# Scan begun under the receptance and gate projections, and the head norm of a key tile placed inside the next tile's product

## The chip, the core and the metric

The kernel runs on one core of one Trainium2 chip. The metric is the device time of one execution in microseconds (us). A core has TensorE (PE, matrix products), VectorE (DVE), ScalarE (ACT) and GpSimd (POOL), which compute, and SyncE (SP), which here only issues DMAs. ACT and POOL issue DMAs too. Each engine works its own instructions in the order written; semaphores are the only links between engines.

## The reference, cut to what matters

The program is two small transformer models in a row. The change lies in one layer of the first, an RWKV-7 layer on 512 image tokens and 256 context tokens of width 1024 (16 heads of 64):

```python
xx = h_shift - h
xr, xw, xk, xv, xa, xg = [h + xx * mix[j] for j in range(6)]
r = xr @ wr
k = xk @ wk
v = xv @ wv
g = sigmoid(xg @ g1) @ g2
kk = to_heads(k * k_k)
kk = kk * rsqrt(sum(kk * kk, axis=-1, keepdims=True) + 1e-12)      # norm per head
for d in range(2):                                                # two directions
    decay = exp(-exp(-softplus(-(w0[d] + tanh(xw @ w1[d]) @ w2[d])) - 0.5))
    a = sigmoid(a0[d] + (xa @ a1[d]) @ a2[d])
    k_d = k * (1.0 + (a - 1.0) * k_a)
...
def step(s, inp):                                                 # the scan over tokens
    r_t, w_t, k_t, v_t, a_t, b_t = inp
    sa = einsum('bhvk,bhk->bhv', s, a_t)
    s = s * w_t + sa[..., None] * b_t[:, :, None, :] + v_t[..., None] * k_t[:, :, None, :]
    return s, einsum('bhvk,bhk->bhv', s, r_t)
```

Before the scan come a Fourier layer and a mixture of experts, after it the output projection, a second mixture of experts and the whole second model. None of these is touched.

## The kernel before, in words

Activations lie transposed: 128 features by tokens, eight such tiles (m = 0 to 7) for the width of 1024. All work of the layer before the scan is the stage `rw`, the scan is the stage `wkv`. Between two stages the helper `phase` makes each of PE, DVE and ACT wait until the other engines have ended the stage (POOL's part too).

Stage `rw` on PE (`rw_tensor`): the decay projection; then for each key tile m the product with `wk` (L986, 16 products written, which the trace counts as 32 matmuls: half have 512 columns, half 256), the four small products of the gate `a` (L998), and the head norm, two products of the squared key with a block matrix of ones (L1006). Then values (L1015, `wv`), receptance (L483, `wr`, eight tiles into the eight PSUM banks), and the output gate: `down("lg", "g1")` (L959) and the product with `g2` (L1027). The inputs of these projections are made by DVE in `mix` (L1070), six times, always into the same tile `XJ`; so each `mix` waits until the projection before it has read `XJ` (`xjfree`).

For a key tile m ACT (`rw_scalar`) copies the product out of PSUM (L1162), squares it (L1169, mark `ksq`), waits for DVE's results of tile m-1 and issues their five stores (L1134, on ACT's own DMA queue), computes two sigmoids of `a` in four instructions (L1175), and takes the square root of the head norm (L1179, mark `rn`). Sigmoid and square root are in different activation tables, so a table load stands before each. DVE (`rw_vector`) then needs the stores of tile m-1 landed and the sigmoids of m, makes the directions' keys (L1103, L1106), takes the reciprocal (L1109), and makes `kk` and its products (L1111, L1114, mark `kout`). PE's head norm waits for `ksq`.

The products of values, receptance and gate are copied out by ACT into staging tiles (L1203, L1206), and POOL stores them to HBM (L1223, L1214).

Stage `wkv` works the tokens in chunks of 64, two units (u, one for each direction) to a step, twelve steps. A unit needs its chunk's streams loaded from HBM into the region of `H` (six DMAs, L1385 on ACT's queue for step 0, L301 on SP's queue for later ones), constants (L1380 to L1382), a cumulative sum on DVE (L1448), exponentials on ACT (L1346, L1347), the scaled keys on DVE (L1458, L1462), the chunk products on PE (L1575, 32 matmuls a unit), their copies on ACT (L1359, L1361), six masks and one strict mask a unit on POOL (L1323, L1337), and a start on DVE (L1484, L1489). Then PE, ACT and DVE go through levels 1 to 5 of a triangular inverse: product L1588, copy L1370, product L1602, addition L1498, transpose L1503. Within a step the next step's sum, exponentials and products are already worked. For step 0 nothing stands before them, so all come one after another when `rw` has ended.

SP loads weights through a ring of eight slots (L2652). Its order is that of `weight_plan`; the first block of `wo` comes after the gate's weights, and `wkv_loads` behind it.

Of the kernel before, what the change touches and what calls it, by code (L numbers as in the profile page):

```python
# [135 lines left out]
def build(nc, a, out, table):  # L136
# [3 lines left out]
    with ctx:  # L140
# [53 lines left out]
        for i in range(5):  # L194
            sems[f"st{i}"] = semaphore(f"stage_tile_{i}_stored_by_pool")
            sems[f"sa{i}"] = semaphore(f"stage_tile_{i}_stored_by_scalar")
        for i in range(2):
# [87 lines left out]
        block = ctx.enter_context(nc.Block())  # L285

# [656 lines left out]
        last_mm = {}  # L943
# [4 lines left out]
        def rw_tensor(pe):  # L948
# [3 lines left out]
            def down(tag, wn, j, last_name):  # L952
                w = weight(pe, wn)
                for s0, sn in jsegs(j):
                    b = bank(pe, f"{tag}.{s0}")
                    for k in range(KT):
                        if later(pe, f"xj{j}.{k}"):
                            pe.wait_ge(*at(f"xj{j}.{k}"))
                        ins = pe.matmul(b[:, 0:sn], w[:, k, :], XJ[:, k, s0:s0 + sn], start=k == 0, stop=k == KT - 1)  # L959
# [18 lines left out]
            wa = weight(pe, "a2")  # L978
            for m in range(KT):
# [9 lines left out]
                if m % 2:  # L989
                    marks[f"wf.wk.{m // 2}"] = (T_, count[T_])  # L990
                for d in range(2):
# [8 lines left out]
                if m == KT - 1:  # L1000
                    marks["xjfree2"] = (T_, count[T_])
                for s0, sn in SEGS:
                    if later(pe, f"ksq.{m}"):
                        pe.wait_ge(*at(f"ksq.{m}"))
                    b = bank(pe, f"kn.{m}.{s0}")
                    did(T_, pe.matmul(b[:, 0:sn], bones[:, :], SQ[:, s0:s0 + sn], start=True, stop=True).then_inc(tensor_done, 1), f"kn.{m}.{s0}")  # L1006
# [14 lines left out]
            down("lg", "g1", 5, None)  # L1021
# [8 lines left out]
        def rw_vector(dve):  # L1030
# [32 lines left out]
            def mix(n):  # L1063
                j = order[n]
                if n:
# [3 lines left out]
                for k in range(KT):  # L1069
                    did(V, dve.scalar_tensor_tensor(XJ[:, k, 0:w], XX[:, k, 0:w], col("mix", 8 * j + k), H[:, k, 0:w],  # L1070
# [46 lines left out]
            mix(5)  # L1117

# [4 lines left out]
        def rw_scalar(act):  # L1123
# [68 lines left out]
            n = 0  # L1192
            for tag in ("v", "r", "g"):
                if tag == "g":
                    lora("lg", 0, ACT.Sigmoid, XSEG)
                for m in range(KT):
# [11 lines left out]
                    n += 1  # L1208

        def rw_pool(pool):  # L1210
# [15 lines left out]
            for tag in ("v", "r", "g"):  # L1226
# [8 lines left out]
            for step in [f"s.{x}.{KT - 1}" for x in ("kk", "kka0", "kka1", "kd0", "kd1")]:  # L1235
                if later(pool, step):
                    pool.wait_ge(*at(step))

# [8 lines left out]
        off = 0  # L1247
# [6 lines left out]
        YA = take_scr(KT, TX)  # L1254
# [5 lines left out]

        AR = [[take_scr(KT, 2, CH) for _ in range(2)],
# [51 lines left out]
        def wkv_pool(pool):  # L1313
# [12 lines left out]
            if later(pool, "wkvc"):  # L1326
                pool.wait_ge(*at("wkvc"))
# [1622 lines left out]
```

## Time and profile before

| | us |
|---|---|
| three runs, median | 4153.48 |
| lowest and highest | 4148.98, 4155.55 |
| the profiled execution, its own time | 4151.23 |
| its span, first to last instruction | 4149.3 |
| stage `rw`, from its first projection to the gate's last product | 1109 to 1467 |
| PE waits between the gate's last product and the first of the scan | 1467 to 1493 |
| scan, from the first chunk product to about | 1493 to 2002 |

The span is 1.9 us shorter than the execution's own time; what lies around it is taken to stay. Positions below are us from the span's start. A row of the timeline gives start, duration, engine, line, operation, what is written and read, and in brackets how long the engine was idle before and who ended that. The mean granted clock of TensorE is 0.956 of full speed, which is 2.4 GHz; the other level is half of it.

### The profile page before, as it was taken

Reading aid. Unit: us, or ns where it says so; the run is one execution under the profiler, and the core shown is the slowest. Engines: PE = TensorE matmul, PEld = TensorE weight load, DVE = VectorE, ACT = ScalarE, POOL = GpSimd, SP = SyncE. Lnnn points to the kernel's source line nnn. Section 1 sums busy time; section 2 is a strip of 40 time slices with the busy share of each in tenths; the row PEclk is TensorE's granted clock in tenths of the full one; section 3 lists DMA queues with packets and bytes.
Section 4 is the critical chain, followed back from the end, with each engine's and each line's share of the span. In section 5 each row is a group of like instructions: output and inputs, shape, how many; then the busy total and the mean of one; then the engine's idle time right before and its main releaser. Section 6 shows DMA issues by size and latency. Waiting matters only on the chain.

```text
span 4149.3 us, 63323 instructions
## 1 busy us (share of the span) xinstructions
PE 3711.9 (89%) x28370; PEld 2288.8 (55%) x28370; DVE 1350.4 (33%) x2376; ACT 1014.9 (24%) x1973; POOL 264.1 (6%) x240
## 2 busy tenths in 40 slices
PE   7998999999698969999768887779989998998998
PEld 3556443434355658888443332235548884656886
DVE  2123000000545047777430000025433332534243
ACT  3012111111232135554210000113323221423231
POOL 0000000000000034434100000000000000000000
PEclk9997999999888989999979999989999999999999
DMA  8345889896034154331519999911122322112230
GB/s 288 102 148 198 304 310 363 307 341 244 33 116 162 42 114 89 69 87 42 174 41 360 375 376 387 384 54 58 51 71 92 92 88 66 55 45 88 91 99 23
DMA packets 530414, 666.74 MB, mean 161 GB/s; under 512 B 156552, under 2 KB 299144, under 8 KB 530144
## 3 DMA queue, kind: packets, MB, share of 16 engines
q1 hardware_dynamic: 506352, 627.37, 44.6%
q10 hardware_dynamic: 19952, 22.81, 1.7%
q0 software_dynamic: 3840, 12.52, 0.8%
q8 instruction: 223, 3.65, 0.4%
q14 instruction: 47, 0.39, 0.0%
HBM read 631.18 MB, written 31.46 MB: 160 GB/s over the span
## 4 chain that ended last, share of the span: by engine, by line
PE 72%; DVE 10%; DMA 6%; SPq 4%; ACT 4%; POOL 2%; ACTq 1%; issue 1%; DVEq 0%; POOLq 0%
PE ps L620 11%; DMA ring<-in_moe_wu 5%; PE ps L625 4%; SPq L2652 4%; PE ps L483 3%; PE ps L813 3%; PE ps L2515 3%; PE ps L2516 3%; PE ps L2517 3%; PE ps L2531 3%; PE ps L2532 3%; PE ps L2530 3%; PE ps L786 3%; PE ps L2151 3%; PE ps L2257 3%; POOL ring L1323 2%
## 5 line engine op out<-in xcount | busy, mean ns | idle before, releaser
L620 PE MATMUL ps<-ring,H 128*64 128x512 f32 x2048 | 494.4, 602 | 52.4 <-DMA ring<-in_moe_wu 39.2
L620 PEld LDWEIGHTS ps<-ring,H 128*64 128x64 f32 x2048 | 146.9, 137 | 343.7 <-issue 253.9
L722 DVE TENSOR_TENSOR scr<-ps,scr 128x512 f32<-128x512 f32 x32 | 22.1, 691 | 965.2 <-PE ps L625 516.9
L620 PE MATMUL ps<-ring,scr 128*64 128x512 f32 x1024 | 248.3, 599 | 39.9 <-DMA ring<-in_moe_wd 38.5
L2515 PE MATMUL ps<-scr_rounded,ring_rounded 128*128 128x512 f32 x512 | 205.0, 400 | 23.0 <-ACT scr_rounded L2553 23.0
L2584 DVE TENSOR_TENSOR ring_rounded<-ring,scr_rounded 128x2048 fp32r<-128x2048 f32 x64 | 146.7, 2292 | 227.6 <-ACT scr_rounded L2550 227.6
L2516 PE MATMUL ps<-H_rounded,scr_rounded 128*128 128x512 f32 x512 | 204.8, 400 | 0.0
L2517 PE MATMUL ps<-scr_rounded 128*128 128x512 f32 x512 | 204.5, 399 | 0.0
L2532 PE MATMUL ps<-scr_rounded 128*128 128x512 f32 x512 | 202.6, 396 | 0.0
L2530 PE MATMUL ps<-scr_rounded,ring_rounded 128*128 128x512 f32 x512 | 202.0, 394 | 0.0
L2550 ACT ACTIVATE scr_rounded<-ring 128x2048 fp32r<-128x2048 f32 x64 | 122.1, 1908 | 257.7 <-PE ps L2532 246.4
L620 PEld LDWEIGHTS ps<-ring,scr 128*64 128x64 f32 x1024 | 73.0, 137 | 188.7 <-issue 125.0
L813 PE MATMUL ps<-scr 128*128 128x512 f32 (+1 forms) x320 | 125.9, 556 | 4.2 <-ACT scr L696 2.9
L786 PE MATMUL ps<-scr 128*128 128x256 f32 x512 | 121.3, 390 | 4.0 <-DVE scr L893 4.0
L2515 PEld LDWEIGHTS ps<-scr_rounded,ring_rounded 128*128 128x128 f32 x512 | 97.6, 191 | 48.5 <-DVE H_rounded L2589 24.6
L625 PE MATMUL ps<-ring,H 128*32 128x256 f32 x2048 | 123.8, 382 | 0.0
L690 ACT ACTIVATE scr<-ps 64x512 f32<-64x512 f32 x64 | 37.8, 591 | 312.6 <-PE ps L625 161.5
L2151 PE MATMUL ps<-H,ring 128*128 128x512 f32 x256 | 111.3, 594 | 0.0
L2516 PEld LDWEIGHTS ps<-H_rounded,scr_rounded 128*128 128x128 f32 x512 | 97.7, 191 | 23.7
L2257 PE MATMUL ps<-scr,ring 128*128 128x512 f32 x256 | 110.7, 593 | 0.0
L2517 PEld LDWEIGHTS ps<-scr_rounded 128*128 128x128 f32 x512 | 97.5, 190 | 23.6
L503 DVE SCALAR_TENSOR_TENSOR X<-ps,ada,X 128x512 f32<-128x512 f32 (+1 forms) x48 | 31.8, 662 | 241.7 <-PE ps L813 127.0
(405 smaller groups left out, 6246.1 us busy)
## 6 DMA issues: line engine op xcount, KB each, us to landing
ring<-in_moe_wg SPq DMA_DIRECT2D x128, 1024.0 KB, 9.2
ring<-in_moe_wu SPq DMA_DIRECT2D x128, 1024.0 KB, 8.4
ring<-in_moe_wd SPq DMA_DIRECT2D x128, 1024.0 KB, 11.3
ring<-in_mlp_w SPq DMA_DIRECT2D x64, 1024.0 KB, 5.5
ring<-in_ada_w SPq DMA_DIRECT2D x48, 1024.0 KB, 8.0
ring<-in_w_in SPq DMA_DIRECT2D x14, 1024.0 KB, 5.2
ring<-in_w_out SPq DMA_DIRECT2D x8, 1024.0 KB, 5.2
st_kka<-scr ACTq DMA_DIRECT2D x16, 384.0 KB, 3.5
```

The source lines that it names most:

```text
L620: ins = pe.matmul(bx[64 * n:64 * n + 64, :], stat_x(k), w[:, k % 4, :], start=k == 0, stop=k == KT - 1)
L625: ins = pe.matmul(bc[32 * n:32 * n + 32, 0:256], stat_c(k), w[:, k % 4, o:o + 256], start=k == 0, stop=k == KT - 1)
L786: ins = pe.matmul(b[:, 0:256], HT[:, tt, k * P:k * P + P], GM[:, tt, :], start=tt == 0, stop=tt == 3)
L813: ins = pe.matmul(b[:, 0:sn], ys[:, j, m * P:m * P + P], sm[:, j, :], start=j == 0, stop=j == nj - 1)
L2151: ins = pe.matmul(b, w[:, k, (m % 2) * P:(m % 2) * P + P], H[:, k, 0:TX], start=k == 0, stop=k == KT - 1)
L2257: ins = pe.matmul(banks[m], w[:, k, (m % 2) * P:(m % 2) * P + P], MIX[:, k, :], start=k == 5, stop=k == 4)
L2515: pe.matmul(b, low[:, k, o], hh, start=k == 0, stop=False)
L2516: pe.matmul(b, high[:, k, o], hl, start=False, stop=False)
L2517: ins = pe.matmul(b, high[:, k, o], hh, start=False, stop=k == KT - 1)
L2530: pe.matmul(banks[m], low[:, k, o], hh, start=f == 0, stop=False)
L2532: ins = pe.matmul(banks[m], high[:, k, o], hh, start=False, stop=f == 15)
L2652: did(f"slot{i % NSLOT}", sp.dma_start(dst, src.rearrange("(k p) c -> p k c", p=min(P, rows))).then_inc(sems[f"slot{i % NSLOT}"], 16), "w. ...
```

## The change

1. Keys: the head norm of tile m-1 (`head_norm`) is written between the 512-column and the 256-column part of tile m's product; that of the last tile stays behind its gate products. The order on ACT and DVE is not changed. The mark that frees `XJ` after the keys is set right after the last key product.
2. `mix` of the gate writes into `XX`, its own input, and so doesn't wait for the receptance projection to end.
3. Loads for step 0 go from ACT's queue to SP's (`wkv_first_loads`), behind the gate's weights and ahead of `wo`: constants once the receptance's inputs are made, the chunk streams once the gate's input is made, the values once the product with `g1` has read `XX`. The stores of the gate's tiles go from POOL to SP, in the same function, and so do the values of step 1.
4. DVE makes sum and scaled keys of step 0 right after `mix` of the gate; ACT makes the exponentials after the third receptance tile (`EXP_AFTER = 2`); PE works both chunk products between receptance and `g1`; ACT copies them out ahead of the gate's sigmoid; POOL masks them behind the stores of the receptance; DVE begins both units.
5. Tiles of the scan get other places in scratch memory, so that those needed early don't overlap what `rw` still uses. `AR` of even steps and of odd steps change places between `X` and scratch.

```diff
@@ wkv_first_loads, new, on SP, called ahead of the plan's "hold.0"
+            if later(sp, "xj5.0"):
+                sp.wait_ge(*at("xj5.0"))
+            did("wkvc", sp.dma_start(RST, a["rst"]).then_inc(sems["wkvc"], 16), by=16)
...
+            if later(sp, f"xj5.{KT - 1}"):
+                sp.wait_ge(*at(f"xj5.{KT - 1}"))
+            steps = list(units())
+            for u, d, c, img, first in steps[0]:
+                for n, s, h in chunk_streams(d, False):
...
+            if later(sp, "lg.0"):
+                sp.wait_ge(*at("lg.0"))
...
+            for u, d, c, img, first in steps[0]:
+                value_loads(sp, u, d, c)
+            for m in range(KT):
+                if later(sp, f"go.{m}"):
+                    sp.wait_ge(*at(f"go.{m}"))
+                did(f"sg{m % 4}", sp.dma_start(*stored("g", m, m % 4, TX)).then_inc(sems[f"sg{m % 4}"], 16), f"s.g.{m}", by=16)
+            for u, d, c, img, first in steps[1]:
+                value_loads(sp, u, d, c)
@@ rw_tensor
+            def head_norm(m):
+                if later(pe, f"ksq.{m}"):
+                    pe.wait_ge(*at(f"ksq.{m}"))
...
                 for s0, sn in SEGS:
+                    if s0 and m:
+                        head_norm(m - 1)
                     b = bank(pe, f"k.{m}.{s0}")
...
-                for s0, sn in SEGS:
-                    if later(pe, f"ksq.{m}"):
-                        pe.wait_ge(*at(f"ksq.{m}"))
...
+            head_norm(KT - 1)
...
-            down("lg", "g1", 5, None)
+            first_step = next(units())
+            chunk_products(pe, *first_step[0])
+            chunk_products(pe, *first_step[1])
+            down("lg", "g1", 5, None, XX)
@@ rw_vector
             mix(5)
...
+            first_step = next(units())
+            for un in first_step:
+                chunk_scan(dve, *un)
+                chunk_tildes(dve, *un)
+            chunk_begin(dve, *first_step[0])
+            if later(dve, "wf.g1"):
+                dve.wait_ge(*at("wf.g1"))
+            chunk_begin(dve, *first_step[1])
@@ rw_scalar
                 if tag == "g":
+                    chunk_evict(act, *first_step[0])
+                    chunk_evict(act, *first_step[1])
                     lora("lg", 0, ACT.Sigmoid, XSEG)
...
+                    if tag == "r" and m == EXP_AFTER:
+                        chunk_exps(act, *first_step[0])
+                        chunk_exps(act, *first_step[1])
@@ rw_pool
-            for tag in ("v", "r", "g"):
+            for tag in ("v", "r"):
...
+            for un in pair:
+                chunk_mask(pool, un, 0)
+                chunk_mask(pool, un, 1)
+            for l in range(2, LEVELS):
+                for un in pair:
+                    chunk_mask(pool, un, l)
+            for un in pair:
+                chunk_strict(pool, *un)
```

PE, the first two key tiles, before: product in two parts (L986), gate products (L998), head norm (L1006).

```order
L986 MATMUL ps<-scr,ring 128x512 x8
L986 MATMUL ps<-scr,ring 128x256 x8
L998 MATMUL ps<-scr,ring 128x512
L998 MATMUL ps<-scr,ring 128x256
L998 MATMUL ps<-scr,ring 128x512
L998 MATMUL ps<-scr,ring 128x256
L1006 MATMUL ps<-scr,bones 128x512
L1006 MATMUL ps<-scr,bones 128x256
L986 MATMUL ps<-scr,ring 128x512 x8
```

The same place in the changed kernel: product L1031, gate products L1045, head norm L1021.

```order
L1031 MATMUL ps<-scr,ring 128x512 x8
L1031 MATMUL ps<-scr,ring 128x256 x8
L1045 MATMUL ps<-scr,ring 128x512
L1045 MATMUL ps<-scr,ring 128x256
L1045 MATMUL ps<-scr,ring 128x512
L1045 MATMUL ps<-scr,ring 128x256
L1031 MATMUL ps<-scr,ring 128x512 x8
L1021 MATMUL ps<-scr,bones 128x512
L1021 MATMUL ps<-scr,bones 128x256
L1031 MATMUL ps<-scr,ring 128x256 x8
```

The head norm of tile 0 now comes after the first eight products of tile 1, and so for each tile.

PE from the values to the scan, before: values L1015, receptance L483, `g1` L959, `g2` L1027, chunk products L1575, level 1 of the scan L1588 and L1602.

```order
L1015 MATMUL ps<-ring,scr 128x256 x192
L483 MATMUL ps<-scr,ring 128x512 x64
L959 MATMUL ps<-scr,ring 128x512 x8
L1027 MATMUL ps<-scr,ring 128x512 x8
L1575 MATMUL ps<-scr 128x64 x32
L1588 MATMUL ps<-scr,ring 64x64 x16
```

The same place after: values L1056, receptance L520, chunk products L1492, `g1` L996, `g2` L1071, level 1 L1648.

```order
L1056 MATMUL ps<-ring,scr 128x256 x192
L520 MATMUL ps<-scr,ring 128x512 x64
L1492 MATMUL ps<-X,scr 128x64 x32
L996 MATMUL ps<-scr,ring 128x512 x8
L1071 MATMUL ps<-scr,ring 128x512 x8
L1648 MATMUL ps<-scr,ring 64x64 x16
```

The chunk products stand ahead of the two gate products instead of behind them.

SP's queue behind the gate's weights, before: `wo`, then the streams of step 1.

```order
L2652 DMA ring<-in_rw_g 128x1024
L2652 DMA ring<-in_rw_wo 128x8x256
L301 DMA H<-st_lw 128x8x64
L301 DMA H<-st_kd 64x8x64 x2
L301 DMA H<-st_kka 64x8x64 x2
L301 DMA H<-st_kk 128x8x64
```

SP's queue there after (L349 are values, L320 the stores of the gate, L338 the streams of step 1; the second stream set of step 0 is left out by the cut).

```order
L298 DMA scr<-in_lm 128x768
L307 DMA H<-st_lw 128x8x64
L307 DMA H<-st_kd 64x8x64 x2
L307 DMA H<-st_kka 64x8x64 x2
L307 DMA H<-st_kk 128x8x64
...
L349 DMA H<-st_v 64x8x64 x2
L349 DMA scr<-st_v 64x8x64 x2
L320 DMA st_g<-scr 128x512 x8
L349 DMA scr<-st_v 64x8x64 x4
L2712 DMA ring<-in_rw_wo 128x8x256
L338 DMA H<-st_lw 128x8x64
```

Ahead of step 1's streams SP now has eight stores that wait for the gate's copies, four value loads and `wo`.

## Rows read from the trace of the kernel before

**Rows 1.** Windows: A:B, length, busy (count) by engine, granted clock, DMA share, GB/s.

```profile
1170.00:1304.00 134.00, 114.93 (x352) 62.80 (x353) 83.40 (x66) 51.98 (x79) 0.00 (x0) 0.93 0.28 106
1467.00:1503.00 36.00, 9.14 (x67) 9.01 (x69) 9.77 (x16) 9.90 (x22) 3.47 (x4) 0.57 1.07 212
```

**Rows 2.** Groups by line, 1170 to 1304: busy, mean ns, idle before, releaser.

```profile
L1006 PE MATMUL ps<-scr,bones 128*128 128x512 f32 (+1 forms) x32 | 17.1, 670 | 13.5 <-ACT scr L1169 13.5
```

**Rows 3.** Chain that ended last, 1170 to 1300: start, us, engine and line.

```profile
1215.99 0.96 ACTq L1134
...
1217.96 1.28 ACT L1175
1219.25 2.00 ACT scr L1175 x4
1221.28 1.28 DVE scr L1103 x2
...
1233.58 0.95 ACTq L1134
```

**Rows 4.** Timeline of PE, ACT and DVE, first key tile.

```profile
1182.79 1.56 PE L1006 MATMUL ps<-scr,bones 128*128 128x512 f32 x4
1184.18 10.48 PE L986 MATMUL ps<-scr,ring 128*128 128x512 f32 x32
...
1185.92 1.05 ACT L1179 ACTIVATE scr<-ps,eps 128x512 f32<-128x512 f32 x2
...
1187.69 4.94 DVE L1109 RECIPROCAL scr<-scr 128x768 f32<-128x768 f32 x1
```

**Rows 5.** Timeline of PE, where the values begin.

```profile
1304.01 5.25 PE L1015 MATMUL ps<-ring,scr 128*128 128x256 f32 x12 [4.95 <-DVE scr L1070]
```

**Rows 6.** Timeline of PE, receptance and the product with g2.

```profile
1395.67 55.17 PE L483 MATMUL ps<-scr,ring 128*128 128x512 f32 x128 [0.94 <-DVE scr L1070]
...
1459.67 7.11 PE L1027 MATMUL ps<-scr,ring 128*128 128x512 f32 x16 [0.78 <-ACT scr L1139]
```

**Rows 7.** Timeline of ACT's queue, DVE and PE, from the gate to level 1.

```profile
1469.07 0.60 ACTq L1385 DMA_DIRECT2D H<-st_lw  x1
...
1481.80 1.22 DVE L1448 TENSOR_TENSOR_SCAN scr<-scr,H 128x512 f32<-128x512 f32 x1 [13.05 <-DMA H<-st_kk]
...
1493.26 9.00 PE L1575 MATMUL ps<-scr 64*128 64x64 f32 x64 [26.49 <-DVE scr L1464]
1502.86 1.97 PE L1588 MATMUL ps<-scr,ring 64*64 64x64 f32 x32 [0.60 <-DVE scr L1489]
```

**Rows 8.** Timeline of PE and DVE in step 0, levels 2 and 3.

```profile
1512.22 1.42 PE L1588 MATMUL ps<-scr,ring 64*64 64x64 f32 x32
...
1516.72 1.15 PE L1588 MATMUL ps<-scr,ring 64*64 64x64 f32 x32 [0.15 <-DVE scr L1503]
...
1527.44 2.60 PE L1575 MATMUL ps<-X,scr 64*128 64x64 f32 x32
...
1518.27 1.18 DVE L1448 TENSOR_TENSOR_SCAN scr<-scr,H 128x512 f32<-128x512 f32 x1
1521.53 0.89 DVE L1498 TENSOR_TENSOR scr<-ps,scr 128x256 f32<-128x256 f32 x2 [2.08 <-PE ps L1602]
```

**Rows 9.** Timeline of POOL, masks of step 0.

```profile
1503.15 12.74 POOL L1323 TENSOR_TENSOR ring<-ring,scr 128x512 f32<-128x512 f32 x10 [1.74 <-ACT ring L1361]
1515.86 2.50 POOL L1337 TENSOR_TENSOR ring<-ring,scr 128x512 f32<-128x512 f32 x2
```

**Rows 10.** DMA issues, 1440 to 1512: KB each, median us to landing.

```profile
ring<-in_rw_wo SPq DMA_DIRECT2D x1, 1024.0 KB, 6.3
...
st_r<-scr POOLq DMA_DIRECT2D x2, 256.0 KB, 2.3
H<-st_lw ACTq DMA_DIRECT2D x2, 256.0 KB, 6.9
...
H<-st_kk SPq DMA_DIRECT2D x2, 256.0 KB, 4.1
```

More of the change, by code:

```diff
@@ new lines, in chunk_evict @@
+        def chunk_evict(act, u, d, c, img, first):
+            sc = SC[u // 2 % 2][d]
+            for b4 in range(4):
+                t = tile(act, f"A{u}.{b4}").rearrange("p (h c) -> p h c", c=128)
+                g, q = divmod(b4, 2)
+                if u >= 4:
+                    if later(act, f"nm{u - 4}.{LEVELS - 1}"):
+                        act.wait_ge(*at(f"nm{u - 4}.{LEVELS - 1}"))
+                    if later(act, f"Q{u - 4}.1"):
+                        act.wait_ge(*at(f"Q{u - 4}.1"))
+                did(A_, act.activation(odd(sc[rows(1 - q), 8 * g:8 * g + 8, :], 1)[:, :, 0:CH],
+                                       t[rows(1 - q), :, 0:CH], ACT.Copy).then_inc(scalar_done, 1))
+                did(A_, act.activation(odd(sc[rows(q), 8 * g:8 * g + 8, :], 0)[:, :, 0:CH],
+                                       t[rows(q), :, 0:CH], ACT.Copy).then_inc(scalar_done, 1), f"nb{u}.{b4}")
+                if not img:
+                    marks[f"free.A{u}.{b4}"] = (A_, count[A_])
@@ new lines, in chunk_products @@
+        def chunk_products(pe, u, d, c, img, first):
+            bk, ar = BK[d], AR[(u // 2) % 2][d]
+            if later(pe, f"til{u}"):
+                pe.wait_ge(*at(f"til{u}"))
+            w = 128 if img else CH
+            for g in range(2):
+                for q in range(2):
+                    b = bank(pe, f"A{u}.{2 * g + q}")
+                    for n, j in enumerate(range(4 * g, 4 * g + 4)):
+                        ins = pe.matmul(b[:, n * 128:n * 128 + w], bk[rows(q), j, :, :],
+                                        ar[rows(q), j, :, :] if img else ar[rows(q), j, 0, :], start=True, stop=True)
+                    did(T_, ins.then_inc(tensor_done, 1), f"A{u}.{2 * g + q}")
@@ L1532, in wkv_vector @@
                 after = steps[n + 1] if n + 1 < NCH else []
-                if now:
+                if n and now:
                     lower(*now[1])
-                    begin(*now[1])
+                    chunk_begin(dve, *now[1])
                 for un in now:
@@ L1544, in wkv_vector @@
                 if after:
-                    scan(*after[0])
+                    chunk_scan(dve, *after[0])
                 for un in now:
@@ L1558, in wkv_vector @@
                 if after:
-                    begin(*after[0])
+                    chunk_begin(dve, *after[0])
         def wkv_tensor(pe):
```

287 lines of the change are left out of this document (136 added, 151 removed).

## The prediction

> **What bounds the kernel now.** I read the views in this order: busy time in windows, to find where TensorE (PE) stands still in the touched stages; then the groups by line, for who ends its waits; then the chain of work that ended last, for whether those waits matter; then the timeline, for the durations. In the scan's opening (1467 to 1503) PE is busy for 9.14 of 36 us [rows 1]: it waits 26.49 us for the first chunk product [rows 7]. In the key loop (1170 to 1304) it is busy for 114.93 of 134 us, and 13.5 us of its idle time stand before the head norm, ended by ScalarE's square [rows 1, 2]. These are the two places the change goes for. They are not alike. In the opening PE waits and nothing else is going on. In the key loop the chain doesn't run over PE at all: from one issue of stores on ACT (1215.99) over the sigmoid's table load, the sigmoids and VectorE's chain to the next issue (1233.58) it is 17.59 us a tile, by ACT, DVE and ACT's queue alone [rows 3]. PE's work for a tile is 114.93/8 = 14.4 us at a mean granted clock of 0.93 [rows 1], or 13.4 at the full one, so PE has 3 to 4 us to spare.
>
> **The head norm.** In steady state nothing is won: the square is issued by ACT at a point that the cycle of 17.59 us sets, and PE's wait of 13.5 us only moves to another place. The norm is still early enough: PE's next product may start once ACT has copied the last one, the norm follows 6.9 us into it (below) and is done some 9 us after that copy; ACT wants it only behind the next sigmoids, and copy and sigmoids lie most of a period apart. So the cycle stays at 17.59 us. But tile 0 has no such slack. Before, its norm ran at 1182.79 and the root on ACT from 1185.92 to 1186.97; the reciprocal began at 1187.69 [rows 4]. Now PE first works 16 matmuls of 512 columns of tile 1: 55.17/128 = 0.431 us each [rows 6], 6.9 us from 1182.8. Then the norm, 1.56, with the first half of its root under the second half: the root ends near 1191.7 and the reciprocal begins at 1191.8 instead of 1187.69. That is **+4.1 us**, and all later tiles follow at 17.59 us each, so it is not given back. The values begin when DVE has made their input after tile 6 (PE idle 4.95, ended by DVE) [rows 5], so they begin 4.1 later too; the earlier mark that frees `XJ` buys nothing, since DVE comes to it later anyway. Bounds: 0, if a wait further on (the stores' landing) takes it up, to 5.5, if the norm's two halves don't overlap with the root. I take 4.1, nearest to that row.
>
> **The opening.** Times are on the scale of before, without the 4.1. Receptance ends at 1450.84 [rows 6]. What must be ready for the chunk products: DVE ends both mixes near 1406; constants and streams are loaded on SP from there. With landings of 4.1 to 6.9 us [rows 10] and sum, exponentials and scaled keys of some 9 us for both units, it is done before 1430: 20 us of cover, the receptance. ACT stands at the exponentials meanwhile, with the copies of receptance tiles queued behind; PE has eight banks for eight tiles and would not notice. If the cover were gone, the whole 9 us and the loads would be on the path.
>
> Then PE: both chunk products at the pace of a busy PE, 2 x 2.60 = 5.2 [rows 8] (before 9.00 for both, at the low clock) [rows 7], `g1` 7.1, sigmoid 0.8, `g2` 7.1 [rows 6]: 20.2, so 1471.1. Beside it POOL: the copies of the second unit end about 0.9 after its products, 1457.0; from there ten masks and two strict masks, 12.74 + 2.50 = 15.3 [rows 9], until 1472.4. The first unit's first two masks, 2.5, fit ahead if the store of the last receptance tile (issued a microsecond after its end, landing in 2.3) [rows 10] has landed at 1454.2; it has. The barrier between the stages waits for POOL, so **level 1 begins at 1472.4** instead of 1502.86 [rows 7]: 30.5 won, less 4.1 = **26.4**. The edits on DVE (both starts) cost nothing: they lie under `g1` and `g2`, 5 us of work in 15; without that cover they would be on the path, as they are now. The other places of tiles cost nothing: the same instructions on tiles of the same size.
>
> **Step 0.** Before, level 1 took from 1502.86 to 1512.22, 9.36 us, with half the masks and the second start still missing and PE at a mean clock of 0.57 until 1503 [rows 1], the low level for most of it. Level 2 took 1516.72 - 1512.22 = 4.5 [rows 8]. Now all is ready, and level 1 should look like level 2: **4.9 won** (bounds 0 and 4.9).
>
> Against it stand the streams of step 1. SP issues them behind the gate's last store, four value loads and `wo`: the gate's last copy ends at 1471.1 + 4.1 + 0.6 = 1475.8, then its store, the loads and `wo` are six issues of 0.60 to 0.65 [rows 7], so from about 1479.7. DVE wants to sum at 1518.27 - 1512.22 = 6.05 after level 2 begins, which is 1476.5 + 4.5 + 6.05 = 1487.1, and has 2.08 us idle behind it [rows 8]: a landing up to 1489.2 is free. Six more issues are over at 1483.6; with 4.1 for the last landing it is 1487.7, with the 12.7 us that step 0's streams took from first issue to the sum (1469.07 to 1481.80) [rows 7] it is 1492.4. So 0 to 3.2; I take **-1.3**, nearer the quiet row, as half of the traffic of that time has gone elsewhere. An activation table is now loaded once more in step 0, since the sigmoid came between: 1.28 at most, half of it hidden by ACT's wait: **-0.5**.
>
> Trace and rule. `wo` takes 6.3 us to land [rows 10], and step 1's streams stand right behind it on SP's queue; before, step 0's streams were on ACT's queue beside it. The Trainium skill (DMA: Bandwidth & Descriptors, Queues, rings and completion order) says each DMA engine consumes one queue's descriptors in ring order, while it alternates between different queues. By that rule the streams start moving only when `wo` is through, and the rival "late streams" below is what happens. No row here has that order on one queue.
>
> Trace and rule again. The sigmoids begin 0.01 us after the table load of 1.28 has ended [rows 3]. The Trainium skill (ScalarE: Activation LUTs, What ACT_TABLE_LOAD costs) adds a drain of about 1.38 us to each switch. By it the extra load would cost 1.4 us more; the rows show no such gap, so I leave it out.
>
> **The sum.** 26.4 + 4.9 - 1.3 - 0.5 = 29.5 us. The span goes from 4149.3 to 4119.8, the profiled execution's own time from 4151.2 to 4121.7; the median of the runs lies 2.3 above that execution, so 4153.5 - 29.5 = **4124.0**. Everything behind step 0 is the same work, moved forward as a whole.
>
> **Rivals.**
> 1. The head norm helps. For it: 13.5 us of waits stand before it [rows 2]. Against: the chain doesn't touch PE [rows 3]. If tile 0's 4.1 is taken up, 4120; if the waits were really on the path, 17.6 more than my sum, 4106.
> 2. Late streams. Loads of step 1 begin only after `wo`: 1479.7 + 6.3 + 12.7 = 1498.7 at the worst, 9.5 after the free point; in the middle 5: 4129, at the worst 4132.
> 3. It doesn't do what it says. POOL's masks start late (a landing, a constant), say only with the gate's end at 1475.2 instead of 1461: the 17.7 us of 14 masks then stand on the path, level 1 at 1492.9 instead of 1476.5, 16.4 lost: 4140.
> 4. Slower than before. PE's idle time is now split into two pieces in each key tile. If the granted clock falls for it (the window's mean is 0.93) [rows 1], PE becomes the bound of the loop: from a mean clock below 13.4/17.6 = 0.76 on. At the low level all through it would be 26.8 us a tile, 9.2 more for seven tiles: +64, 4188. Against it: the same idle time per tile as before.
>
> **How the numbers follow.** Forecast 0.60 (4119 to 4128 by its bounds), rival 1 0.12, rival 2 0.17, rival 3 0.07, rival 4 0.04. The range 4114 to 4134 takes in the forecast, rival 2 and the near half of rival 1. A difference of 0.2% (8 us) is about what a measurement tells from no change; only rival 4 reaches the slower side: faster 0.94, no difference 0.02, slower 0.04.
>
> **What would show it.** Right: in the key loop a period of 17.6 us, PE's waits moved but as long, the reciprocal of tile 0 near 1191.8, the values at 1308; no idle PE over 2 us from receptance to level 1; level 1 near 1476.5, ended by POOL's last mask; level 2 4.5 later. Wrong: values at 1304 or earlier (rival 1); DVE's first sum in step 0 ended by a DMA (rival 2); PE idle over 5 us ahead of level 1 (rival 3); a granted clock under 0.76 in the key loop (rival 4).

## The result, and the profile after

The changed kernel takes 4122.32 us (median of 4 runs, 4117.20 to 4125.04), the kernel before 4152.67 beside it (4 runs, 4148.98 to 4155.55). The ratio is 0.9926, with a 95% interval of 0.9909 to 0.9943: 30.35 us by the medians, where 29.5 were forecast. The profiled execution of the changed kernel has a span of 4119.5 us against 4149.3 (forecast 4119.8), and a mean granted clock of 0.961.

The windows, in the same form as [rows 1]: the key loop, and the opening from the last receptance tile to level 1.

```profile
1170.00:1304.00 134.00, 117.25 (x352) 63.09 (x352) 80.76 (x62) 51.81 (x79) 0.00 (x0) 0.94 0.26 98
1451.00:1480.00 29.00, 25.09 (x201) 14.54 (x200) 5.46 (x7) 14.09 (x31) 18.65 (x15) 1.00 0.40 123
```

In the opening PE is now busy for 25.09 of 29 us at full clock, where it was busy for 9.14 of 36 at 0.57. The key loop looks as before. Its details stand in the timeline of DVE and ACT, first key tile (answers to [rows 4]):

```profile
1169.38 7.52 DVE L1115 SCALAR_TENSOR_TENSOR scr<-scr,vec,H 128x768 f32<-128x768 f32 x8 [12.10 <-PE ps L996]
...
1190.99 1.05 ACT L1240 ACTIVATE scr<-ps,eps 128x512 f32<-128x512 f32 x2 [4.89 <-PE ps L1021]
...
1192.08 4.95 DVE L1154 RECIPROCAL scr<-scr 128x768 f32<-128x768 f32 x1 [4.11 <-ACT scr L1240]
```

The reciprocal of tile 0 (L1154) now waits 4.11 us for the root of the head norm. It begins at 1192.08; 1191.8 was forecast. The period from one reciprocal to the next is 17.60 us behind it. The eight mixes of the keys (L1115) are the origin used further down, since whole executions lie a few us apart by then: 1169.19 before, 1169.38 here.

Timeline of PE from the values to step 0 (answers to [rows 5 to 8]):

```profile
1306.97 5.30 PE L1056 MATMUL ps<-ring,scr 128*128 128x256 f32 x12 [4.94 <-DVE scr L1115]
...
1399.42 55.17 PE L520 MATMUL ps<-scr,ring 128*128 128x512 f32 x128 [0.94 <-DVE scr L1115]
1454.52 4.61 PE L1492 MATMUL ps<-X,scr 64*128 64x64 f32 x64
1459.06 7.13 PE L996 MATMUL ps<-scr,ring 128*128 128x512 f32 x16
1466.97 7.10 PE L1071 MATMUL ps<-scr,ring 128*128 128x512 f32 x16 [0.78 <-ACT scr L1200]
1477.20 1.15 PE L1648 MATMUL ps<-scr,ring 64*64 64x64 f32 x32 [3.13 <-POOL ring L1410]
...
1481.21 1.15 PE L1648 MATMUL ps<-scr,ring 64*64 64x64 f32 x32
...
1485.75 1.15 PE L1648 MATMUL ps<-scr,ring 64*64 64x64 f32 x32
```

Both chunk products take 4.61 us behind the receptance, 9.00 before. Level 1 (L1648) begins at 1477.20, after 3.13 us of waiting for POOL's last strict mask (L1410); 1476.5 and that releaser were forecast. One of the forecast's signs is not met: it had no idle PE over 2 us between receptance and level 1, and here it is 3.13, since `g2` ends at 1474.07 and not at 1475.2, and POOL is later than thought. It takes 4.01 us to level 2 and 4.54 to level 3.

Timeline of POOL and of DVE there (answers to [rows 8, 9]):

```profile
1458.95 15.67 POOL L1405 TENSOR_TENSOR ring<-ring,scr 128x512 f32<-128x512 f32 x12 [2.83 <-ACT ring L1431]
1474.57 2.48 POOL L1410 TENSOR_TENSOR ring<-ring,scr 128x512 f32<-128x512 f32 x2
...
1489.27 1.22 DVE L1451 TENSOR_TENSOR_SCAN scr<-scr,H 128x512 f32<-128x512 f32 x1 [1.80 <-DMA H<-st_kk]
1490.56 0.89 DVE L1576 TENSOR_TENSOR scr<-ps,scr 128x256 f32<-128x256 f32 x2
```

POOL works 18.1 us without a pause. DVE's first sum for step 1 (L1451) is ended by a DMA, 1.80 us late; the addition behind it (L1576) begins 4.81 us after level 3 (1485.75), as before (1521.53 - 1516.72) [rows 8], so nothing was lost by it.

### The profile page after: what moved, and what is told of

Same layout as the page of the kernel before. It is cut to its first block, busy times and chain, and to the rows that moved or that the text cites. A ratio compares the mean times of both kernels' runs of the same rounds, so it can differ in the third digit from the quotient of the medians.

```text
span 4119.5 us, 63325 instructions
## 1 busy us (share of the span) xinstructions
PE 3706.1 (90%) x28370; PEld 2280.0 (55%) x28370; DVE 1350.7 (33%) x2376; ACT 1016.0 (25%) x1974; POOL 260.6 (6%) x232
## 4 chain that ended last, share of the span: by engine, by line
PE 73%; DVE 10%; DMA 5%; ACT 4%; SPq 4%; POOL 2%; issue 1%; ACTq 1%; DVEq 0%; POOLq 0%
PE ps L657 12%; PE ps L662 4%; DMA ring<-in_moe_wu 4%; SPq L2712 4%; PE ps L520 3%; PE ps L850 3%; PE ps L2573 3%; PE ps L2574 3%; PE ps L2575 3%; PE ps L2589 3%; PE ps L2590 3%; PE ps L2588 3%; PE ps L823 3%; PE ps L2209 3%; PE ps L2315 3%; POOL ring L1405 2%
```

## The experiments

Three stretches tell the runs apart. A: from the mixes of the keys to the receptance. B: from the receptance to level 1. C: from level 1 to step 0's last products. B begins with the receptance's first product, C with that of level 1. Each of these is one profiled execution's (norm_only's B is 1508.68 - 1401.38, and so on). A ratio's interval is against runs of the kernel before on the same chip. The intervals reach some 5 to 7 us to either side (norm_only's 4), so differences of 2 or 3 us can't be told from the medians. In A and B kernels that are alike in that stretch agree within some 0.4 us, but for a stretch of low clock in A (below). C scatters more: undo_norm, norm0_first, split_new, split_old and products_late are written in step 0 as the changed kernel is, which has 31.11, and have 31.66 to 33.90. A difference of up to 2.8 us in C is therefore not read as an effect here.

| kernel | time, median | ratio, 95% | A | B | C |
|---|---|---|---|---|---|
| before | 4152.67 | | 226.48 | 107.19 | 35.36 |
| changed | 4122.32 | 0.9909 to 0.9943 | 230.04 | 77.78 | 31.11 |
| norm_only | 4152.89 | 0.9990 to 1.0009 | 229.80 | 107.30 | 35.38 |
| undo_norm | 4119.71 | 0.9906 to 0.9936 | 226.79 | 77.44 | 32.62 |
| norm0_first | 4120.92 | 0.9908 to 0.9938 | 224.04 | 77.78 | 32.93 |
| products_late | 4134.94 | 0.9948 to 0.9974 | 227.88 | 92.13 | 31.66 |
| exps_last | 4133.67 | 0.9943 to 0.9972 | 229.82 | 87.88 | 34.21 |
| strict_late | 4120.39 | 0.9906 to 0.9943 | 229.82 | 75.45 | 36.53 |
| streams_wait | 4125.04 | 0.9921 to 0.9953 | 229.75 | 77.45 | 34.75 |
| streams_first | 4123.23 | 0.9915 to 0.9944 | 229.83 | 77.43 | 33.81 |
| strict_streams | 4120.90 | 0.9902 to 0.9936 | 229.97 | 75.45 | 30.93 |
| split_new | 4094.11 | 0.9846 to 0.9875 | 198.94 | 77.44 | 33.90 |
| split_old | 4090.66 | 0.9836 to 0.9865 | 196.26 | 77.44 | 31.77 |
| best_all | 4088.51 | 0.9832 to 0.9865 | 196.25 | 75.45 | 31.45 |

### The two halves apart: norm_only and undo_norm

norm_only is the kernel before with the moved head norm alone; undo_norm is the changed kernel with the norm back in its place.

```diff
-                    if s0 and m:
-                        head_norm(m - 1)
...
+                head_norm(m)
```

> The kernel before with the moved head norm alone. Theory 1: later by 3 to 4 us at the start of the receptance (1399.4 instead of 1395.67), span 4152 to 4153.5, a difference in the runs too small to measure. Theory 2: up to 13.5 us faster, span 4136 to 4149.

> The changed kernel with the head norm back behind its own tile's gate products; all else as changed. Theory 1 (the key loop's chain runs over ScalarE, VectorE and ScalarE's queue, so the moved norm only delays tile 0): the reciprocal of tile 0 begins near 1187.8 instead of 1192.08, the values near 1304 instead of 1306.97, the receptance near 1395.7 instead of 1399.42, and the span is 2.8 to 3.8 us shorter than that of the changed kernel: about 4116. Theory 2 (the wait in front of the norm was on the path and the change took it away): the span is longer, by up to 13.5 us: 4120 to 4133.

The moved norm alone wins nothing: ratio 1.0. It lengthens stretch A by 3.3 us and leaves B and C as they were (norm_only against before). Taken out of the changed kernel it gives 3.25 us back in A. All that the change wins is therefore in B and C: 29.4 and 4.25 us, less 3.6 in A. Undo_norm's C is 1.5 us longer, which is within the scatter. The difference of the medians for the norm, 2.6 us here, can't be told from nothing by itself.

### Only tile 0: norm0_first

The changed kernel, with the head norm of tile 0 in its old place and the other seven inside the next product.

```diff
-                    if s0 and m:
+                    if s0 and m > 1:
...
+                if m == 0:
+                    head_norm(0)
```

> The changed kernel with the head norm of key tile 0 back in its old place and the other seven inside the next product. Theory 1 (only tile 0 has no slack, the other norms have 3 us and more): the reciprocal of tile 0 begins 3.1 us behind the square-plus-sigmoid part as before, i.e. without idle time on DVE; that of tile 1 comes 19.07 us after it, as before, because DVE waits there for the landing of st_kd; then 17.6 us each; values and level 1 3.0 to 3.6 us earlier than in the changed kernel as counted from the stage's start: 4119 to 4120 (ratio 0.992). Rival F (each of the moved norms costs or wins something): the tiles' period differs from 17.6, and the values begin at another distance than 0.3 us from the version with all norms in place.

DVE, the reciprocals of tiles 0 and 1 in it:

```profile
1188.69 4.94 DVE L1156 RECIPROCAL scr<-scr 128x768 f32<-128x768 f32 x1
...
1206.29 4.95 DVE L1156 RECIPROCAL scr<-scr 128x768 f32<-128x768 f32 x1
```

The mixes begin at 1170.19 in this run, so the reciprocal of tile 0 is 18.50 us behind them, exactly as before (1187.69 - 1169.19): the 4.1 us are tile 0's. But tile 1 comes 17.60 us later and not 19.05 as it did before, and the values begin 133.40 us behind the mixes: 1.4 less than before, 4.2 less than in the changed kernel (137.59). The expectation had taken the longer first period as a property of the loop, and its figures for tile 1 and the values did not come. It isn't one. In the kernel before DVE waited for the stores of tile 0:

```profile
1203.69 1.27 DVE L1103 TENSOR_SCALAR scr<-scr,vec,small 128x768 f32<-128x768 f32 x2 [8.14 <-DMA st_kd<-scr]
```

They took 5.7 us to land there, against 3.9 in the changed kernel, in norm_only and in norm0_first. The DMA view of the kernel before for 1197 to 1199 (queue, kind: packets, MB, share), and what the 16 engines moved from 1201 to 1204 (GB/s in 40 slices), show what else went on (an "instruction" packet is a load of program code for an engine):

```profile
q8 instruction: 1, 0.02, 2.9%
```

```profile
GB/s 246 573 328 410 205 82 41 0 41 41 0 41 41 0 41 0 41 41 0 41 41 0 41 41 0 41 0 41 0 0 0 0 0 0 0 0 0 0 0 0
```

One load of instructions fell on one of the 16 DMA engines while the stores were under way. From 1201.5 on a single engine is still at work, at a steady trickle until 1203, and the store counts as landed when its last part has. In the changed kernel the same load comes at 1194, in norm0_first at 1195, before their stores; in undo_norm at 1199, again among them, and there the stores take 5.7 us as well. In all nine kernels with the stores on ACT and some norm moved, the load comes some 25 us behind the mixes, before the stores, and tile 1 follows tile 0 by 17.6 us. In before and undo_norm it comes 29 us behind them, among the stores, and tile 1 follows by 19.05. So a third of what the norm's new place costs tile 0 comes back (1.45 of 4.2 us). The likely cause is that a code load and a store no longer meet; no run moved the load alone. The rest of norm0_first's lead in A (2.4 us against before, 1.4 of them so far) is in the second half of the values. Its 256 matmuls took 57.21 us in the changed kernel and before, where the granted clock fell to 0.50 for some 2 us near the start, and 55.52 in norm0_first and products_late, where it stayed at 1.00; against that 1.7, norm0_first waited 0.7 longer ahead of them (2.90 us for 2.23).

### What bounds the opening: products_late and exps_last

products_late puts the chunk products behind `g2` and their copies behind the gate's; loads, sums, exponentials and scaled keys stay early.

```diff
-            chunk_products(pe, *first_step[0])
-            chunk_products(pe, *first_step[1])
             down("lg", "g1", 5, None, XX)
...
             marks["wf.g2"] = (T_, count[T_])
+            chunk_products(pe, *first_step[0])
+            chunk_products(pe, *first_step[1])
```

> The changed kernel, but PE works the two chunk products behind the product with g2, and ScalarE copies them out behind its gate copies; loads, sums, exponentials and scaled keys stay early. Theory 1 (in the opening all hangs on GpSimd's 14 masks, 18.2 us from the first to the end, and so on the time at which the chunk products are copied out): g2 ends near 1469.5, the products near 1474, the first mask begins near 1474.3, the last strict mask ends near 1492.4 and level 1 begins there instead of at 1477.20: +15 us, some 4137 (ratio to the kernel before 0.9964). Rival A (what was won is the early loads, sums and exponentials; the masks would lie beside the scan's levels, as they did in part before): level 1 begins right behind the copies, near 1479 to 1482, 4124 to 4127 (0.994).

```profile
1465.57 4.61 PE L1492 MATMUL ps<-X,scr 64*128 64x64 f32 x64
1487.84 1.97 PE L1648 MATMUL ps<-scr,ring 64*64 64x64 f32 x32 [17.67 <-POOL ring L1410]
```

PE stands 17.67 us before level 1, for POOL's last mask. Stretch B grows by 14.35 us (15 expected), the time by 12.6. Had only the early loads and sums counted (rival A), level 1 would have come right behind the copies. What the early products buy is an early start of POOL's masks. They are half of what B gained: from 107.19 to 92.13 it is the work that products_late keeps early (loads, sums, exponentials, scaled keys) with PE at the full clock in the products, 15.1 us; from there to 77.78 it is the products ahead of the gate, 14.35.

exps_last takes the cover away from the exponentials (`EXP_AFTER = 7` for 2), so that they stand behind the last receptance tile.

```diff
-        EXP_AFTER = 2
+        EXP_AFTER = 7
```

> The changed kernel with EXP_AFTER = 7: the exponentials of step 0 stand behind the last copy of the receptance instead of the third, so they and the scaled keys lose their cover. Theory 1: exponentials from 1455.3, with table load, second sum and both sets of scaled keys the second product begins near 1465 and g1 near 1467.3 instead of 1459.06; copies end near 1469.3, POOL's last mask near 1485, level 1 there instead of 1477.20: +8 us, 4130 (ratio 0.9946). Rival B (the gate's 15 us of PE and POOL's masks have room for it): level 1 still near 1477 to 1479, 4122 to 4124 (0.993).

```profile
1460.54 9.09 PE L1492 MATMUL ps<-X,scr 64*128 64x64 f32 x64 [5.22 <-DVE scr L1467]
1469.56 9.79 PE L996 MATMUL ps<-scr,ring 128*128 128x512 f32 x16
1480.13 7.10 PE L1071 MATMUL ps<-scr,ring 128*128 128x512 f32 x16 [0.78 <-ACT scr L1200]
1488.03 1.15 PE L1648 MATMUL ps<-scr,ring 64*64 64x64 f32 x32 [0.79 <-issue]
```

The windows of it, over the chunk products and over `g1`:

```profile
1460.50:1470.00 9.50, 9.46 (x65) 9.34 (x66) 5.53 (x7) 6.66 (x17) 2.49 (x2) 0.50 0.00 1
1469.56:1480.00 10.44, 9.79 (x17) 3.94 (x16) 1.08 (x2) 2.63 (x4) 9.47 (x8) 0.74 0.00 0
```

Stretch B is 10.1 us longer; 8 were expected. POOL's part came as expected: its last mask ended at 1485.71, 7.9 us later against the receptance. But it was not the last. After the wait of 5.22 us PE worked at the lower clock (0.50, that is 1.2 GHz): the products took 9.09 us instead of 4.61 and `g1` 9.79 instead of 7.13. So level 1 waited for the gate's own products and copies (the last ended at 1487.93), 2.3 us behind POOL. C is 3.1 us longer too: DVE's sum for step 1 waited 5.27 us for `st_kk`, and PE 3.33 us before level 4. The time went up by 11.4 us.

### The end of the opening: strict masks and the streams of step 1

strict_late moves the two strict masks from the end of `rw_pool` to the start of `wkv_pool`, behind the barrier.

```diff
@@ rw_pool
-            for un in pair:
-                chunk_strict(pool, *un)
@@ wkv_pool
+            for un in next(units()):
+                chunk_strict(pool, *un)
```

> The changed kernel with the two strict masks of step 0 moved behind the barrier, into the scan's own list of POOL. Theory 1 (the barrier waits for POOL's last mask alone, and by 2.4 us more than for the next): level 1 begins at 1474.9, behind ScalarE's last gate copy (1474.77), instead of 1477.20; the strict masks run beside level 1 and nobody wants them before step 0's last products: -2.3 us, 4120 (ratio 0.992). Rival C (something behind POOL is late as well, a store or load): level 1 stays within 0.5 us of 1477.2, 4122.

```profile
1472.85 1.15 PE L1648 MATMUL ps<-scr,ring 64*64 64x64 f32 x32 [0.79 <-ACT scr L1270]
...
1489.87 1.23 DVE L1449 TENSOR_TENSOR_SCAN scr<-scr,H 128x512 f32<-128x512 f32 x1 [6.76 <-DMA H<-st_kk]
```

B shrinks by 2.33 us, ended by ACT's last gate copy, as forecast to 0.1. In the profiled execution all of it is lost: the sum now waits 6.76 us for `st_kk`, PE stands 4.82 us before level 4, and C is 5.4 us longer. The median of the runs, 4120.39, is where the theory had put it (4120), and the profiled execution (4126.38) was the slowest of four; so how much of the loss every execution has is not shown. On SP the last four value loads took 4.35 us to issue (2.57 in the changed kernel), so `wo` and the streams behind it didn't move forward with the rest, and SP issued a unit's six streams in 7.9 us. The theory of one bound was too simple; the streams stood just behind it. Why the value loads were slow to issue is open.

streams_wait lets SP wait until `wo` has landed before it issues the streams.

```diff
                 if name == "wo.1":
+                    if later(sp, "w.wo.0"):
+                        sp.wait_ge(*at("w.wo.0"))
                     wkv_loads(sp)
```

> The changed kernel with SP waiting until the first block of wo has landed before it issues the streams of step 1: the full case of 'streams only behind wo'. In the changed kernel DVE's first sum of step 1 waited 1.80 us for st_kk (to 1489.27) and nothing came of it, since its next addition stood at 1490.56, 4.81 us behind level 3 as before. Theory 1 (slack is used up at just that point): wo lands 1484 to 1486, the streams land near 1494, the sum begins there, and the addition of level 3 and all behind it move by 5 to 6 us: 4128 (ratio 0.994). Rival D (stream loads have slack anyway, or wo's landing is quick): sum within 1 us of 1489.3, 4122 (0.9926). If wo is slow to land (8.9 us, the median of the four blocks), +8: 4130.

The sum waits 5.10 us instead of 1.80, C is 3.6 us longer (5 to 6 expected; `wo` landed in 6.4 us, and the streams were then issued faster). The time is 2.7 us up, which by itself can't be told from nothing. PE waits 3.15 us before level 4 in it, where the changed kernel has no wait. So there is hardly any slack behind the 1.80: in the changed kernel the sum ends at 1490.49, and the addition behind it begins at 1490.56.

streams_first issues them ahead of `wo`, strict_streams does both, best_all does both on the fastest version (below).

```diff
                 if name == "hold.0":
                     wkv_first_loads(sp)
+                    wkv_loads(sp, 1, 2)
...
                 if name == "wo.1":
-                    wkv_loads(sp)
+                    wkv_loads(sp, 2, 99)
```

> The changed kernel with the streams of step 1 issued ahead of the first block of wo instead of behind it. Theory 1 (in the changed kernel these streams arrive just in time: DVE's sum was 1.8 us late, and that was idle time anyway): the sum waits for nothing (DVE idle 0 before it), level 4 begins 14.8 to 15.0 us behind level 1 as before, the time stays within 1 us of the changed kernel, 4121 to 4122 (ratio to before 0.9925). Rival D (the streams behind wo hold back step 0): 1.5 to 3 us won, 4119 to 4120.

> Both: the two strict masks of step 0 behind the barrier, and the streams of step 1 ahead of wo. With the masks alone level 1 came 2.55 us earlier against the stage's start, but DVE's sum then waited 6.76 us for st_kk (1.80 in the changed kernel) and step 0's last products came 2.9 us later. Theory 2 (the masks' gain is real and was lost to the streams behind wo): sum without a wait over 1 us, level 1 2.4 us earlier and step 0's last products 2.4 us earlier than in the changed kernel, 4120 (0.992), and 3 to 5 us less time up to step 0's last products than with the masks alone. Rival E (something else held the sum, as the gate's stores, which these streams wait for in both): sum still waits 3 us or more and nothing is won against the changed kernel, 4122 to 4125.

In streams_first the sum waits 0.30 us, level 4 begins 14.87 us behind level 1, and no gain follows, as theory 1 said. C is even 2.7 us longer than in the changed kernel, for another reason, which is also part of C's scatter. PE's timeline of it, in level 4:

```profile
1495.03 0.50 PE L1662 MATMUL ps<-ring 64*64 64x64 f32 x10 [2.29 <-issue]
1495.46 3.92 PE L1492 MATMUL ps<-scr 64*128 64x64 f32 x32
```

PE stands 2.29 us between the 22nd and the 23rd of 32 products of one group, waiting for nothing that the profile shows (`issue`), and works at half clock after it (granted clock 0.50 from 1499.3 to 1503). Such a gap in the same group is 0.65 us in the changed kernel, 0.89 in undo_norm, 0.92 in norm0_first, and absent in strict_streams and products_late; split_new has one of 1.95 in level 3. No semaphore stands there. A load of instructions runs 1 to 3 us before each of these gaps, but such loads come every 4 to 6 us in strict_streams and products_late too, where no gap follows. PE may have waited for its code; no row names whose code it was, so this stays open.

In strict_streams the sum waits 2.99 us instead of 6.76, B is 2.33 us shorter and C 0.18 shorter than in the changed kernel: 2.5 us won up to step 0's last products, where strict_late had lost 3.1. The 2.33 of B are clear; C differs from strict_late's by 5.6 us, twice the scatter, and from the changed kernel's by nothing that can be told. So theory 2 holds in the stretches of these two executions, except that the sum was to wait under 1 us; here too the value loads were slow to issue (3.77). The medians of the runs don't show it: 4120.39 for the masks alone, 4120.90 for both, 4122.32 for the changed kernel.

### The bound of the key loop: split_new and split_old

The chain of a key tile [rows 3] runs from ACT's issue of five stores to the next. Here POOL issues them, the two of `kd` as soon as they are made, and DVE waits for those two apart from the other three. ACT still waits for DVE's results of tile m-1 ahead of the sigmoids, but no longer issues five stores between the two. split_new has the norm inside the next product, split_old in its old place.

```diff
@@ rw_scalar
-                    store_keys(m - 1)
+                    if later(act, f"kout.{m - 1}"):
+                        act.wait_ge(*at(f"kout.{m - 1}"))
@@ rw_pool
+            for m in range(KT):
+                for mark, part in ((f"kdo.{m}", ((3, "kd0"), (4, "kd1"))), (f"kout.{m}", ((0, "kk"), (1, "kka0"), (2, "kka1")))):
...
+                        did(f"sk{s}", pool.dma_start(*stored(stream, m, s, TA)).then_inc(sems[f"sk{s}"], 16), f"s.{stream}.{m}", by=16)
```

> The changed kernel with the five key stores issued by GpSimd instead of ScalarE, those of kd as soon as they are made and waited for apart from the other three. That takes the stores' issue (3.3 us) and their landing off the cycle of a key tile. Theory 1: the cycle becomes sigmoids 2.0 + VectorE's chain 10.9 = 13.0 us, under TensorE's 13.4, so the period falls from 17.6 to about 13.4 us and the span by 7 x 4.2 = 29 us at most, 22 to 29 with the ends of the loop: 4091 to 4098. Theory 2 (the loop is bound by TensorE's order and waits): the period stays over 16 us and the span gains under 10 us.

> The same key stores on GpSimd, with the head norm back in its old place. Tells whether the norm inside the next product is worth something once TensorE is near the bound. Theory 1: in the old place the norm waits for a square that follows the last root, about 6 us into the period, and TensorE's order from norm to norm is as long as its work, 13.4 us; the two placements come out within 3 us a loop of each other, the old one ahead by the 4 us of tile 0: 4088 to 4096. Rival: in the old place TensorE idles 2 us or more a tile in front of the norm, and the kernel is 10 us or more slower than with the norm moved.

The window of the key loop in split_new, and PE's groups in split_old from 1200 to 1280:

```profile
1170.00:1304.00 134.00, 129.72 (x444) 76.87 (x445) 101.19 (x80) 58.95 (x91) 21.36 (x40) 0.99 0.45 165
```

```profile
L1031 PE MATMUL ps<-scr,ring 128*128 128x512 f32 (+1 forms) x192 | 62.9, 486 | 0.0
...
L1023 PE MATMUL ps<-scr,bones 128*128 128x512 f32 (+1 forms) x25 | 9.9, 515 | 0.0
```

The period falls from 17.60 to 13.32 us a tile: PE's own work, 13.4 in the prediction's estimate, with no idle time left. With the norm in either place that is worth 28 to 29 us (4122.32 to 4094.11 with it moved, 4119.71 to 4090.66 with it in the old place), about as much as the change itself (30.35). How it divides between the issue (3.3 us a tile on ACT), the stores' landing and the earlier stores of `kd` is not shown: the three went together. And even here, where PE is the bound, the norm in its old place waits for nothing (idle 0.0) and stretch A is 2.7 us shorter with it; the medians, 4090.66 against 4094.11, agree but can't tell.

> The version with the key stores on GpSimd's queue and the head norm in its old place (4090.66), with the strict masks behind the barrier and the streams of step 1 ahead of wo. Theory 2: 2.4 us less than without the two: 4088 (ratio 0.9845). Rival E: no change, 4090.7 (0.9851).

best_all has as short a B as strict_late and strict_streams (75.45) and, with 4088.51 us (4084.41 to 4098.65, 4 runs; ratio 0.9849), the lowest median; against split_old the 2.1 us are as forecast and within the noise; in the stretches B is 2.0 shorter. It beats both kernels of this case, by 64 and 34 us.

## Why the prediction was right, point by point

**What bounds the kernel.** The opening was PE waiting for a chain that no product of PE covered: B fell by 29.4 us. The key loop was not bound by PE: norm_only won nothing, and taking the stores off ACT's queue took 4.3 us from each tile, until PE was the bound. Both readings of [rows 1 to 3] hold.

**The head norm, +4.1.** The size at its place is right: the reciprocal of tile 0 is 4.2 us later against the mixes. "All later tiles follow at 17.59 us each, so it is not given back" is the step that failed. 1.45 us came back at tile 1, whose period had been 19.05 in the kernel before, where a code load fell among the stores; the values are 2.8 us later and the receptance 3.6, not 4.1. The 0.8 between the two is a wait in the middle of the values, 3.01 us for 2.23, which the forecast didn't have; so 3.6 is near 4.1 in part by luck. The row with 19.05 stood in the trace, and was passed over. A bound for this had been given (0, if the landing of the stores takes it up), with the right mechanism.

**The opening, 26.4.** Level 1 at 1477.20 instead of 1502.86 is 25.7 us, with POOL's last mask as the releaser. The 0.7 that is missing: the second unit's copies ended 6.55 us behind the receptance and not 6.16, 0.4 late; the first unit's two masks (until 1461.56) outlasted them (1461.14) by another 0.4; the ten masks behind them took 13.0 us and not 12.74, but the forecast had rounded its sum up (12.74 + 2.50 is 15.24, and 1457.0 + 15.24 is 1472.2, not 1472.4), so only 0.1 of that shows; PE began 0.15 behind POOL; the origin lies 0.2 later; and A gave 0.5 back, as told. products_late shows the mechanism (+14.35 of 15), exps_last the cover under the receptance, and that without it the clock falls too.

**Step 0, 4.9 for level 1.** 9.36 - 4.01 = 5.35 us, better than the bound of 4.9. Level 1 is 0.5 shorter than level 2, since its second unit's product begins 0.95 us behind the first (1478.15), where in level 2 it is 1.45 (1482.66), after a wait for DVE's transpose. No run isolates this term; it is read from the two traces.

**Late streams, -1.3, and the table load, -0.5.** The streams came at 1489.27, the free point had been put at 1489.2: the wait was real and hidden. The extra table load (1.28 us, from 1491.10) cost next to nothing: level 4 follows level 3 by 6.38 us, before by 6.33. The exponential behind it begins at 1492.39, 0.01 us after its end, so the further 1.4 us that the forecast named and left out did not come. What did cost were things that were not in the sum: the gaps of 0.22 and 0.65 in PE and 3.01 instead of 2.60 for a chunk product after them. From level 2 to the last products step 0 takes 27.10 us against 26.00, so 1.1 lost in all where 1.8 were allowed.

**The sum.** 25.7 + 5.35 - 1.1 = 29.9 us at step 0's last products (1538.22 to 1508.31), and 29.8 in the span; 29.5 had been forecast. The errors are small and partly cancel (-0.7 in the opening, +0.45 in level 1, +0.7 behind it), and that the sum came nearer than its terms is luck.

**The rivals.** "The head norm helps" fell: it costs 3.3 us of A in norm_only. "It doesn't do what it says" is what products_late looks like, and isn't this kernel. The clock in the key loop stayed at 0.94. "Late streams" was nearest: its sign, a sum ended by a DMA, is there, without a price. Behind `wo` (issued 1477.77, landed after 6.9, at 1484.7) the first stream took 6.1 us, to 1484.8; with `wo` behind it, in streams_first, 4.2. By the Trainium skill (DMA: Bandwidth & Descriptors, Queues, rings and completion order) each DMA engine consumes one queue's descriptors in ring order. The trace agrees with that. It doesn't agree with what the prediction made of it, that the streams start moving only when `wo` is through: the stream's 256 KB can't have moved in the 0.1 us between the two landings, while all engines together moved 255 GB/s, which is some 30 KB. The price stayed small because SP needed until 1485.80 to issue a unit's six streams anyway, and the last landed in its usual 4.1. In strict_late, with the same order, C was 5.4 us longer in the one execution that was profiled.

## What to carry to other kernels

Work that stands before a barrier pays only down to the next thing that must be there: in the profiled execution of strict_late the strict masks' 2.3 us were lost again, since the streams behind them had no slack left (0.07 us). The runs' medians don't decide whether this is so in every execution. A wait that one engine shows (13.5 us before the head norm) says nothing of its price: find the cycle that sets the period, and there the issue of DMAs counts as work of the engine that does it, and so do the waits in front of it. When the period of one tile differs from the others in the trace of before, ask why before counting on it.

## What was not expected of the hardware

- With a single load of instructions (0.02 MB) on one of the 16 DMA engines a store of 384 KB took 1.8 us longer to land (5.7 against 3.9): one engine worked on until 1203 where the others had ended by 1201.5. So it was in both kernels in which the two met, and in none in which they didn't; that the load is the cause is inferred. With a product moved the load came some 25 us behind the mixes instead of 29.
- After a wait of 5.22 us PE's granted clock was 0.50 over 9.5 us and 0.74 over the next 10.4. After waits of 2.2 to 3.0 us before the second half of the values it sometimes fell to 0.50 for some 2 us (57.21 us for 256 matmuls) and sometimes not (55.52 after a wait of 2.55 or 2.90), in kernels that are alike up to there. The same at level 1: after 3.13 us of waiting the clock stayed at 1.00 in the changed kernel and was 0.50 in norm0_first (1472.9 to 1476.3).
- PE stood for 0.65 to 2.29 us in the middle of a group of products with no semaphore, in five of the kernels. It is not settled what it waited for.
- SP took 7.1 us to issue six loads behind `wo` in the changed kernel (DMA share 1.00 from 1478.70 to 1485.80) and 5.1 with `wo` landed, in streams_wait (0.75 from 1484.90 to 1490.00). The issue was slower where the engines were fuller; no run tests whether that is the cause.
